# Five attention phases with transposes two units behind the scores and values three

## The reference, cut to what matters

```python
# first block, on h = rmsnorm(x), m = rmsnorm(mem)
p = softmax(sc - slopes * dist); a = p[:, :, 0] - lam * p[:, :, 1]; o = a @ v   # diff_attention: 8 heads, two maps each
p = softmax(concat([sc - slopes * dist, sinks]))[..., :span]; o = p @ v         # window_attention: 16 heads, 4 kv heads
p = softmax(q @ mk.T / 16); o = p @ mv                                          # memory_attention: 4 heads of 256
merged = gate0 * (o_da @ w_da_o) + gate1 * (o_wa @ w_wa_o) + gate2 * (o_xa @ w_xa_o)
# then 16 experts (expert_choice_ffn)
# second block, two layers: q, k with rope; layer 0 a causal window with sinks, layer 1 block attention
# (with 256 tokens plain causal attention); o * silu(z); h + o @ w_out
# third block: feed-forward, gated and recurrent layers (not touched)
```

## Time and profile before

| what | value |
|---|---|
| median of three runs | 2952.09 us |
| the profiled execution | 2953.87 us |
| its span, first to last instruction | 2951.8 us (2.1 us lie around it) |
| PE busy | 2449.3 us (83%) |
| DVE busy | 1239.5 us (42%) |
| ACT busy | 970.2 us (33%) |
| mean granted TensorE clock | 0.885 of full |

### The profile page before, as it was taken

The page is one execution under the profiler, slowest core; times in us unless marked ns, Lnnn a source line. Parts: engine busy times, 40 slices in busy tenths (PEclk is TensorE's granted clock), DMA queues, the critical chain, the costliest instruction groups (busy, mean ns, idle before and its releaser), DMA issues.

```text
span 2951.8 us, 39522 instructions
## 1 busy us (share of the span) xinstructions
PE 2449.3 (83%) x17250; PEld 1737.1 (59%) x17250; DVE 1239.5 (42%) x1754; ACT 970.2 (33%) x1545; POOL 62.2 (2%) x36
## 2 busy tenths in 40 slices
PE   6998997767667666666588879999999998887998
PEld 6998896211111111111277768889788887776787
DVE  4466653100001000000255655567654656655654
ACT  4456642000000000000145454444544443643442
POOL 0000010000000000000000000000000000023000
PEclk8999998876776776777698999999999999999999
DMA  5553366999999999999533336565555554321552
GB/s 193 171 155 106 127 212 237 417 418 418 416 416 418 418 418 415 417 418 418 203 112 101 115 100 214 186 210 189 200 196 183 192 186 143 110 97 59 172 181 105
DMA packets 326316, 698.19 MB, mean 237 GB/s; under 512 B 35424, under 2 KB 244576, under 8 KB 291456
## 3 DMA queue, kind: packets, MB, share of 16 engines
q1 hardware_dynamic: 322688, 679.32, 62.1%
q0 software_dynamic: 2016, 13.67, 1.2%
q10 hardware_dynamic: 1440, 2.68, 0.2%
HBM read 694.58 MB, written 1.05 MB: 236 GB/s over the span
## 4 chain that ended last, share of the span: by engine, by line
PE 59%; DMA 27%; DVE 8%; ACT 4%; issue 1%; ACTq 0%; POOL 0%; DVEq 0%; SPq 0%
PE ps L540 16%; PE ps L542 15%; PE ps L541 15%; DMA af<-in_w_exp_gate 12%; DMA af<-in_w_exp_up 10%; DMA af<-in_w_exp_down 6%; PE ps L1418 2%; PE ps L1449 1%; DVE ar L526 1%; PE ps L2144 1%; PE ps L766 1%; PE ps L1037 1%; PE ps L887 1%; PE ps L1761 1%; ACT ar L505 1%
## 5 line engine op out<-in xcount | busy, mean ns | idle before, releaser
L540 PE MATMUL ps<-ar 128*128 128x256 f32 (+1 forms) x2944 | 993.1, 337 | 70.5 <-DVE ar L526 41.0
L541 PE MATMUL ps<-ar 128*128 128x256 f32 (+1 forms) x2944 | 974.1, 331 | 0.0
L542 PE MATMUL ps<-ar 128*128 128x256 f32 (+1 forms) x2944 | 973.9, 331 | 0.0
L526 DVE TENSOR_TENSOR ar<-af,ar 128x1024 fp32r<-128x1024 f32 x520 | 612.2, 1229 | 340.2 <-ACT ar L505 340.1
L540 PEld LDWEIGHTS ps<-ar 128*128 128x128 f32 x2944 | 571.6, 194 | 139.7 <-DVE ar L526 43.3
L541 PEld LDWEIGHTS ps<-ar 128*128 128x128 f32 x2944 | 572.7, 195 | 46.9 <-issue 0.5
L542 PEld LDWEIGHTS ps<-ar 128*128 128x128 f32 x2944 | 571.4, 194 | 48.6
L505 ACT ACTIVATE ar<-af 128x1024 fp32r<-128x1024 f32 x520 | 515.0, 1049 | 153.1 <-PE ps L542 150.5
L1418 PE MATMUL ps<-af 128*32 128x512 f32 x2048 | 367.6, 815 | 183.9 <-DMA af<-in_w_exp_gate 92.2
L1418 PEld LDWEIGHTS ps<-af 128*32 128x32 f32 x2048 | 50.5, 124 | 486.8 <-DMA af<-in_w_exp_up 234.7
L1449 PE MATMUL ps<-af 128*32 128x512 f32 x1024 | 176.9, 805 | 97.9 <-DMA af<-in_w_exp_down 83.9
(11 more groups left out here) (279 smaller groups left out, 1636.9 us busy)
## 6 DMA issues: line engine op xcount, KB each, us to landing
af<-in_w_exp_gate SPq DMA_DIRECT2D x128, 1024.0 KB, 25.5
af<-in_w_exp_up SPq DMA_DIRECT2D x128, 1024.0 KB, 24.9
af<-in_w_exp_down SPq DMA_DIRECT2D x128, 1024.0 KB, 21.5
af<-in_ffn_w_in SPq DMA_DIRECT2D x88, 1024.0 KB, 5.7
af<-in_ffn_w_out SPq DMA_DIRECT2D x44, 1024.0 KB, 5.1
af<-in_w_in SPq DMA_DIRECT2D x33, 1024.0 KB, 5.1
af<-in_sgu_w_in SPq DMA_DIRECT2D x16, 1024.0 KB, 7.5
af<-in_w_out SPq DMA_DIRECT2D x12, 1024.0 KB, 5.0
```

What stands on the lines that cost most here:

```text
L526: e.tensor_tensor(self.WL[load.pair][:, c], self.base(i)[:, c], f_(self.WH[load.pair][:, c]), ALU.subtract).then_inc(*self.dve.inc(("lo", ...
L540: e.matmul(o, lh, rh, start=start, stop=False, skip_group_check=True)
L541: e.matmul(o, lh, rl, start=False, stop=False, skip_group_check=True)
L542: return e.matmul(o, ll, rh, start=False, stop=stop, skip_group_check=True)
```

## The change

The three generators get one more step of lag. Step i now holds, on PE, scores i, transposes i-2, values i-3; on DVE, x and max of i first and then n of i-1; on ACT, e of i first, then p of i-2, then o of i-3. There are two places for the transposed maps (`ptw` becomes two tensors, the second in unit 40 of the SBUF arena), so p of i waits for v of i-2 instead of v of i-1; the PSUM banks of the scores (2, 3) and of the transposes (4, 5) stay single. The generators yield 24 (6) times instead of 26 (8), and the ratios are set to that. In the second block three query blocks come before the attention and one inside.

```diff
-        for i in range(n):
-            ...
-            t.then_inc(*self.pe.inc(("ps", name, "s", i)))
-            yield
-            if i:
-                transposes(i - 1)
-            yield
-            if i:
-                values(e, i - 1)
+        for i in range(n + 3):
+            if i < n:
+                ...
+                t.then_inc(*self.pe.inc(("ps", name, "s", i)))
                 yield
-        ...
+            if 2 <= i < n + 2:
+                transposes(i - 2)
+                yield
+            if i >= 3:
+                values(e, i - 3)
+                yield
@@ a_attention
-                for w in self.Aw.new(self.pe.val(("ps", name, "pt", i, m)), *([self.pe.val(("ps", name, "v", i - 1))] if i else [])):
+                for w in self.Aw.new(self.pe.val(("ps", name, "pt", i, m)), *([self.pe.val(("ps", name, "v", i - 2))] if i > 1 else [])):
@@ v_attention
-        for i in range(n):
-            if i:
-                normed(i - 1)
+        def mapped(i):
...
+        for i in range(n + 3):
+            if i < n:
+                mapped(i)
+                if i:
+                    normed(i - 1)
                 yield
@@ t_second, a_second and v_second alike
-            run(dense_q(0, 2))
+            run(dense_q(0, 3))
...
-                yield from dense_q(2, 4)
+                yield from dense_q(3, 4)
...
-                  dense_z(), 26, 16)
+                  dense_z(), 24, 13)
```

More of the change, by code:

```diff
@@ L888, in transposes, with PT @@
                 t.then_inc(*self.pe.inc(("ps", name, "pt", i, m)))
-        for i in range(n):
[L891 to L897, removed]
-            t.then_inc(*self.pe.inc(("ps", name, "s", i)))
-            yield
-            if i:
-                transposes(i - 1)
-            yield
-            if i:
-                values(e, i - 1)
-                yield
[L906 to L913, removed]
+        for i in range(n + 3):
+            if i < n:
+                free = self.take(2, (name, "s", i), (self.dve, (name, "x", i)))
+                free += self.take(3, (name, "s2", i), (self.dve, (name, "x", i)))
+                for qt in range(2):
+                    for m in range(2):
+                        for w in self.Tw.new(*free, *ready(i)):
+                            e.wait_ge(*w)
+                        t = scores(e, i, m, qt, self.ps[:, 2 + m, at[qt]])
+                t.then_inc(*self.pe.inc(("ps", name, "s", i)))
+                yield
+            if 2 <= i < n + 2:
[4 more added lines that the diff above has]
+                yield
+    def PT(self, i):
+        return self.ptw[i % 2].rearrange("p (m c) -> p m c", m=2)
     def a_attention(self, e, name, n, sink, maps, out, causal=False):
@@ L945, in a_attention @@
[L945 to L949, removed]
+                e.activation(self.PT(i)[:, m, 0:at[1].stop], self.ps[:, 4 + m, 0:at[1].stop], ACT.Copy).then_inc(*self.act.inc((name, "p", i, m)))
+        for i in range(n + 3):
+            if i < n:
+                X, st = self.maps_at(i), self.ST[:, i % 4, :]
+                for g in range(4):
+                    d = X[:, g // 2, at[g % 2]]
+                    for w in self.Aw.new(self.dve.val((name, "max", i))):
+                        e.wait_ge(*w)
+                    e.activation(d, d, ACT.Exp, bias=st[:, g:g + 1],
+                                 accum_out=st[:, 4 + g:5 + g]).then_inc(*self.act.inc((name, "e", i, g)))
+                if sink:
+                    for w in self.Aw.new(self.dve.val((name, "sink", i))):
+                        e.wait_ge(*w)
+                    e.activation(st[:, 12:16], st[:, 12:16], ACT.Exp).then_inc(*self.act.inc((name, "e", i, 4)))
+                yield
+            if 2 <= i < n + 2:
+                places(i - 2)
+                yield
+            if i >= 3:
+                out(e, i - 3)
+                yield
@@ L1023, in v_attention @@
                                 ALU.add).then_inc(*dve.inc((name, "sink", i)))
-            yield
-            yield
-            if i:
-                yield
[L1028 to L1031, removed]
+        for i in range(n + 3):
+            if i < n:
+                mapped(i)
+                if i:
+                    normed(i - 1)
+                yield
+            if 2 <= i < n + 2:
+                if i == n:
+                    normed(n - 1)
+                yield
+            if i >= 3:
+                yield
     def score_pair(self, q, k, causal=False):
@@ L1124, in t_mix @@
                                self.t_pv_pair("wa", OB, lambda i, kt: self.wav[:, kt, i // 2 * 64:i // 2 * 64 + 64]),
-                               lambda i: self.over("wa_in") if i == 0 else []), dense_b(), 26, 25)
+                               lambda i: self.over("wa_in") if i == 0 else []), dense_b(), 24, 25)
         self.end(self.pe, "xa_in")
@@ L1149, in dense_c @@
             yield from self.t_proj(e, "wa_o", 4, both(self.op, F), self.halves("wa"), DB, self.by_dve("wa_o"))
-        weave(self.t_attention(e, "xa", 2, xa_scores, 2, xa_values, lambda i: self.over("xa_in") if i == 0 else []), dense_c(), 8, 17)
+        weave(self.t_attention(e, "xa", 2, xa_scores, 2, xa_values, lambda i: self.over("xa_in") if i == 0 else []), dense_c(), 6, 17)
         self.end(self.pe, "xo_in")
```

46 lines of the change are left out of this document (13 added, 33 removed).

## The result

The change is slower: 2966.14 us (median of four runs, 2965.22 to 2969.71) beside 2949.91 for the kernel before, ratio 1.0053, 95% interval 1.0037 to 1.0070. That is 16 us more, where 12 more were forecast. The profiled execution has a span of 2963.2 us, 11.4 over that of before, and a mean granted clock of 0.883.

The account below looks back on a forecast made before the run. PE was taken to bound da, wa and xa, and to wait in att0 and att1, paced by the ACT-DVE round. Terms 3.0 + 4.5 + 1.1 + 3.0 + 0.5 = +12 us gave 2964 us, range 2946 to 2975.

Parts of the forecast that it names:

- The round: Middle of att0, ACT and DVE from x to next x: 10.1 us against 9.5 before, setting the pace.
- the point that decides: In att0 and att1 the round must fall under PE's 8.5 us for the lag to work.
- The entry: Start of att0 and att1: PE idles 4.6 and 4.0 us ahead of scores 2, which wait for x 1.
- without a wait for a division: Sign in the profile after: att0 and att1 reach their ends with no wait for a division.
- The sum for `att0`: att0: waits 17.1 us against 10.4, low-clock loss 3.5 against 7.2, together +3.0 us.
- For `att1`: att1: waits 11.9 us against 8.9, low-clock loss 3.0 against 5.5, together +0.5 us.
- The bounds beside the sum: att0 and att1: -3.5 us each if no low-clock loss shows, +6 and +3 with all of it as before.
- nothing won: Entry of att0 and att1: moving the third q block (6.1 us) ahead leaves the 2.1 us wait before unit 0.
- `da` and `wa`: First block's phases: new PE waits, da +3.0 us (range 0 to +5), wa +4.5 us (0 to +7).
- It comes out even: Rival: da and wa have unseen slack or low-clock loss is absorbed whole; 2946 to 2958 us, chance 0.22.
- the lag does what it says: Rival: divisions leave PE's path in att0 and att1, about 20 us won, 2932; chance 0.11 for under 2946.
- more low clock: Rival: each of six waits over 2 us also drops the clock, +8 us more, 2972 to 2980; chance 0.09.

Follow-up runs that it names:

- second_only: Lag and moved third q block only in att0 and att1, da, wa and xa as in the kernel before: 2958.78 us, ratio 1.0026.
- e_back: The change with e of unit 2 and later back in its unit's second step on ACT: 2946.88 us, ratio 0.9977.
- q_alone: The kernel before with only the third q block moved ahead of the attention in the second block: 2968.86 us, ratio 1.0063.
- mix_only: The lag only in da, wa and xa, the second block as in the kernel before: 2959.35 us, ratio 1.0028.
- late1_q3: The change with e in its unit's second step for all units, and units 0, 1, 2 taking 2, 3, 3 steps: 2932.94 us, ratio 0.9943.

## Why the prediction was right, and where it was not

*Sign and size* were right: +16 measured, +12 forecast, inside the forecast case of 2958 to 2972. By the single terms it is less good: `second_only` lost 7.9 us where the terms of the second block give 3.5, and that the total came near is in part luck.

*The round.* The one that was worked out came true to 0.1 us, and so did its make-up: Silu and p between e and the high parts. The comparison with before did not. "9.5" is the time from transposes to transposes; from the x of that round (1546.58) to the next (1555.85) it was 9.27, and x was not on the old chain. By the averages above the round is 9.80 us against 9.96, not longer. What holds of "the round sets the pace" is shown by `e_back`: a shorter round, 8.82 us, and 19 us less. The prediction even named the point that decides, "Silu and p would have to run beside DVE's low parts; the order of ACT above speaks against it". `e_back` makes just that order, by one step of e, and the lag then wins, with a ratio of 0.9977. What the prediction didn't say is that this order is no consequence of the lag. It took the change as one piece, and gave the pipeline's depth a verdict that belongs to one yield.

*The entry* was right in place and nearly in size: PE waits 3.4 us in `att0` and 3.7 in `att1` for x 1 ahead of scores 2 (4.6 and 4.0 forecast). In `att0` the rotation of the third block then waits 1.1 us (2.9 forecast) and transposes 1 wait 1.9 for rope (1.4 forecast). The start as a whole is worth 14 us over all phases. The late waits of `att0` were 3.5 us for p, as forecast, and 2.6 for a division (4.2 for p forecast), so the sign "without a wait for a division" failed there.

*The sum for `att0`* came out at +2.9 for +3.0, by two errors that cancel. The waits within the phase were 12.9 us, not 17.1, so 2.5 more than before in place of 6.7; but the loss to the low clock, taken as what the waits leave over, did not fall by 3.7 us as the sum had it, it stayed about the same (2.9 - 2.5). *For `att1`* they didn't cancel: +3.5 for +0.5. Waits were 10.6 (forecast 11.9), 1.7 more than before, and 1.8 us were lost in addition where 2.5 were to be won. This is the term that was mis-sized. The mean clock agrees: 0.88 against 0.95 in the earlier trace rows. The bounds beside the sum were off too: no loss at all gives -0.5 and -2.5, not "-3.5 each", and the loss of before gives +6.7 in `att0`. The argument "PE idles more, but the dense halves behind the waits end inside the next wait" has no support in these windows.

*The moved `q` block*, "nothing won", was the wrong step: alone it loses 18 us, and with the lag and the spread start it wins 13. What it does with the bunched start no run shows. The step rested on the one wait at the entry, which indeed stayed (4.5 us in 2), and not on what the block had covered inside the phase. The sum still came out near since the lag took the divisions off PE's path: of the 23.8 us of `q_alone` 2.6 are left in the change.

*`da` and `wa`.* In the profile 5.1 and 6.1 us against 3.0 and 4.5 forecast, `xa` 0.9 against 1.1; by the runs of `mix_only` all three are 8.4 against 8.6. A single profile is less sure than that: in that of `mix_only`, with the same `da`, it took 1.5 us more than in the change. In `da` PE waits 2.35 us, 21 us after the first scores; forecast were 2.2 at that place. e 2 and the low part ended there within 0.1 us of the forecast, and the copy of a dense result (L741), also queued behind e 2 on ACT, 0.1 us after the low part. Three later waits of 0.7 us stand for the two of 0.4. `e_back` takes this mechanism away from unit 2 on: there `da` is 1.1 us over before, not 5.1. In `wa` the waits were forecast nearly one by one: 0.8, 0.6, 1.1, 1.6 and 3.0 us, 7.1 in all for 7.2. The terms then add up to +4.8, not +4.5; where the rest of the 6.1 lies no run shows.

*The rivals.* "It comes out even" and "the lag does what it says" fell for this change. The third, more low clock, was there as a part (the clocks of 0.89 and 0.88) but not to its 2972. Not every new wait dropped the clock (see the last section).

*Left open:* how the 14 us of the start divide between the phases, which only the profiles split (`att0` 3.1, `att1` 6.2, the rest in `wa`).

## What to carry to other kernels

When engines run in a fixed order, put an instruction in the step where its input is ready, not in the step where its unit begins: each early instruction makes its wait everybody's wait on that engine. If a deeper pipeline loses time, list the waits of the helper engines before and after; a wait that has changed from "for the engine that sets the pace" to "for another helper" names the instruction to move. And ask of work that is moved out of a phase what it had covered there: the same block cost 18 us in one order and won 13 in another.

## What the runs showed of the hardware

The mean granted clock did not follow PE's idle time. In `att1` PE idles 14.3 us of the window before (76.70 - 62.37) and 14.7 after (73.30 - 58.62), and the mean clock is 0.95 and 0.88: by an estimate from these means, with the low level at half speed, about 7.7 and 17.6 us were spent there. (The window before also holds the third `q` block.) In `late1_q3` only 8.1 us are idle (63.80 - 55.70) and the clock is 0.92. Nor does the length of one wait decide it. The wait ahead of the first scores is 2.1 us before and 2.2 in the change; the 2 or 3 us behind it ran at a granted clock of 1.00 before and of 0.50 in the change. Of the later waits of `att1` in the change, those of 3.65, 2.20 and 2.29 us were followed by stretches at 0.50 to 0.52, that of 2.26 us by one at 1.00. Why, no run shows. A sum over waits alone doesn't give this loss; the prediction missed it by some 4 us in each of the two phases.

The rows also show that here a table load doesn't wait with the instruction it stands ahead of. Of the next unit, in the change:

```profile
1561.67 1.28 ACT L930 ACT_TABLE_LOAD   x1
```

The x of that unit starts only at 1562.82 (the round above), so the load is over before there are maxima, and hidden in e's wait. In `e_back`, where ACT comes to e later, the load stands on ACT's path between p and e: the maxima end at 1542.92 and e starts at 1543.97, 1 us that PE covers.
